# The first rows of the mixers' output product run under the long convolution, and product streams take in weights across their borders

## The reference, cut to what matters

```python
h = rms_norm_2(x, norm_g[l, 0])
q, k, v, g, lr, u_f, u_h, u_s = jnp.split(h @ w_in[l], split_at, axis=-1)
y_a = gla_mixer(q, k, v, g, lr, ...)                     # linear attention
y_b = rms_norm_2(fnet_mixer(u_f), grp_norm_g[l, 0])      # Fourier mixer
y_c = rms_norm_2(hyena_mixer(u_h, ...), grp_norm_g[l, 1])   # two long convolutions
y_d = rms_norm_2(shortconv_mixer(u_s, ...), grp_norm_g[l, 2])
mix = jnp.concatenate([y_a, y_b, y_c, y_d], axis=-1)     # 4 x 512 columns
x = x + mix @ w_out[l]
x = x + cross_attention(rms_norm_2(x, ...), rms_norm_2(mem, mem_norm_g), w_xq, w_xkv, w_xo)
x = x + swiglu(rms_norm_2(x, norm_g[l, 2]), w_gate_up, w_down)
```

## Time and profile before

| what | value |
|---|---|
| median of three runs | 4070.18 us (4068.68 to 4078.13) |
| profiled execution | 4056.73 us |
| its span | 4054.9 us |
| TensorE busy | 3645.2 us, 90% |
| VectorE busy | 1987.7 us, 49% |
| ScalarE busy | 1517.0 us, 37% |
| mean granted TensorE clock | 0.948 of full speed |
| read from memory | 523.28 MB, 131 GB/s over the span |

### The profile page before, as it was taken

How to read it: one execution, slowest core, us unless ns; L and a number is a source line. 1 busy time by engine, 2 the same in 40 slices (tenths; PEclk the granted TensorE clock), 3 DMA queues, 4 the chain that set the end, 5 groups by cost and what they waited for, 6 DMA issues and landing times. The chain is left out here.

```text
span 4054.9 us, 73903 instructions
## 1 busy us (share of the span) xinstructions
PE 3645.2 (90%) x32796; PEld 2991.7 (74%) x32796; DVE 1987.7 (49%) x3429; ACT 1517.0 (37%) x2562; POOL 271.3 (7%) x321
## 2 busy tenths in 40 slices
PE   7899999999999978969989787968999989999998
PEld 3576676776777756847778677826889889999887
DVE  1444454444544455374565446545544455555444
ACT  1333333333433332154444343324443344444343
POOL 0011110100101130021000000010000000000000
PEclk8899999999999989979999799979999999999999
DMA  9523323333232343223225343305554445555554
GB/s 326 179 60 103 99 80 112 103 99 117 83 112 78 103 142 109 70 96 104 94 91 184 108 154 115 104 21 172 169 189 146 156 148 186 183 183 185 187 187 156
DMA packets 343100, 536.18 MB, mean 132 GB/s; under 512 B 11484, under 2 KB 119676, under 8 KB 340604
## 3 DMA queue, kind: packets, MB, share of 16 engines
q1 hardware_dynamic: 340476, 527.25, 40.4%
q10 hardware_dynamic: 2304, 4.20, 0.3%
HBM read 523.28 MB, written 8.13 MB: 131 GB/s over the span
## 5 line engine op out<-in xcount | busy, mean ns | idle before, releaser
L300 PE MATMUL lane<-r,r 128*128 128x256 f32 (+1 forms) x8664 | 1554.9, 328 | 31.7 <-DVE r L258 16.8
L300 PEld LDWEIGHTS lane<-r,r 128*128 128x128 f32 x8664 | 1300.7, 190 | 215.4 <-issue 24.8
L300 PE MATMUL bank<-r,r 128*128 128x512 f32 (+2 forms) x6216 | 1363.6, 357 | 54.8 <-DVE r L258 44.3
L258 DVE TENSOR_TENSOR r<-ring,r 128x1024 fp32r<-128x1024 f32 x749 | 913.7, 1227 | 998.1 <-ACT r L297 997.1
L300 PEld LDWEIGHTS bank<-r,r 128*128 128x128 f32 x6216 | 1016.8, 195 | 259.0 <-issue 65.1
L297 ACT ACTIVATE r<-ring 128x1024 fp32r<-128x1024 f32 x749 | 785.8, 1056 | 1070.6 <-PE lane L300 683.5
L300 PE MATMUL lane<-arena 64*64 64x64 f32 (+5 forms) x13676 | 663.2, 250 | 90.4 <-DVE arena L258 33.5
L300 PEld LDWEIGHTS lane<-arena 64*64 64x64 f32 (+2 forms) x13676 | 502.8, 140 | 239.7 <-issue 124.0
L297 ACT ACTIVATE arena<-lane 128x256 f32<-128x256 f32 (+4 forms) x575 | 251.4, 456 | 582.9 <-PE lane L300 482.5
L269 DVE COPY arena<-lane 128x256 f32<-128x256 f32 (+2 forms) x365 | 131.5, 362 | 335.4 <-PE lane L300 332.3
L258 DVE TENSOR_TENSOR arena<-arena 128x256 f32<-128x256 f32 (+6 forms) x546 | 241.9, 475 | 33.6 <-ACT arena L297 13.7
(11 more groups left out here) (101 smaller groups left out, 1385.6 us busy)
## 6 DMA issues: line engine op xcount, KB each, us to landing
ring<-in_mod_w SPq DMA_DIRECT2D x96, 1024.0 KB, 5.3
ring<-in_w_gate_up SPq DMA_DIRECT2D x88, 1024.0 KB, 5.1
ring<-in_ev_w_in SPq DMA_DIRECT2D x44, 1024.0 KB, 8.6
ring<-in_w_down SPq DMA_DIRECT2D x44, 1024.0 KB, 5.1
ring<-in_od_w_in SPq DMA_DIRECT2D x40, 1024.0 KB, 5.1
ring<-in_w_in SPq DMA_DIRECT2D x40, 1024.0 KB, 5.2
ring<-in_w_xkv SPq DMA_DIRECT2D x32, 1024.0 KB, 5.2
ring<-in_ev_w_out SPq DMA_DIRECT2D x16, 1024.0 KB, 5.1
```

The costliest lines, as they stand in the source:

```text
L258: return Nothing() if self.e is None else self.e.tensor_tensor(o, a, b, op)
L300: return Nothing() if self.e is None else self.e.matmul(o, l, r, start=start, stop=stop)
```

## The change

- **Streams share one list of waiting units.** `stream` now only appends its units to `waiting`. Whoever runs a unit first prepares up to three waiting units, of whichever stream. The calls of `stream` stand earlier in the order, ahead of the drain of the stream before, at seven borders: before attention's input product, the linear attention's inputs, the inputs of short conv and Fourier mixer, the long convolution's inputs, the output product, the queries, and the feed-forward part. The stream of keys and values is created after the output product's units have all been placed.
- **The output product begins in the long convolution.** Its contraction now starts with mix tile 12 (`rot` 12: tiles 12 to 15, 0 to 7, then 8 to 11). Of column groups 0 and 1 the first twelve contraction tiles, 12 units in all, come first and are placed at the yields of the new generator `hyena()`. The tile splits of the mix that they need are placed there too.
- **Buffers and loads.** Instead of the fence "hyena" only a mark is set, on which SyncE's `hy_load` and ScalarE's mix splits wait. The high parts of the mix lie where the input rows were. The convolution takes its banks from four (4 to 7) and not eight. `load_ahead(6)` asks for three pieces of output weights ahead of `hy_load`. `load_mem` stands before the filters' transforms, goes to a place of its own (`M.memx`), and waits for no fence.

```diff
-    M.mF = Pair("mF", at(MF, 4096), at(GAP, 4096), KT, R)
+    M.mF = Pair("mF", at(MF, 4096), at(0, 4096), KT, R)
...
+    M.memx = at(4096, 4096).rearrange("p (t n) -> p t n", t=2)
...
-    def stream(groups, turn):
-        units = []
-        for g in groups:
+    waiting, ahead = [], [0]
+
+    def stream(groups, turn, first=(0, 0)):
+
+
+
+        stretches = [(g, k0, i >= first[0] or k0 >= first[1]) for i, g in enumerate(groups)
+                     for k0 in range(0, g.kt, 2 * min(g.kt, PIECE // 2 // g.n))]
+        count = 0
+        for g, k0, _ in sorted(stretches, key=lambda s: s[2]):
+            g.turn = turn
             hk = min(g.kt, PIECE // 2 // g.n)
-            for k0 in range(0, g.kt, 2 * hk):
-                m2 = min(2 * hk, g.kt - k0)
-                for h in range(0, m2, hk):
-                    units.append(Unit(g, k0 + h, min(hk, m2 - h), h, h + hk >= m2, numbers[0]))
-                    numbers[0] += 1
-                    units[-1].whole = (k0, m2)
-        at_hand = [None]
-
-        def prepare(u):
-            g = u.group
-            if u.half == 0:
...
-        for u in units[:2]:
-            prepare(u)
+            m2 = min(2 * hk, g.kt - k0)
+            for h in range(0, m2, hk):
+                u = Unit(g, k0 + h, min(hk, m2 - h), h, h + hk >= m2, numbers[0])
+                numbers[0] += 1
+                u.whole = (k0, m2)
+                waiting.append(u)
+                count += 1
 
         def run():
-            for i, u in enumerate(units):
-                if i + 2 < len(units):
-                    prepare(units[i + 2])
+            for _ in range(count):
+                while ahead[0] < min(3, len(waiting)):
+                    prepare(waiting[ahead[0]])
+                    ahead[0] += 1
+                u = waiting.pop(0)
+                ahead[0] -= 1
                 products(u)
                 for _ in range(CHORES[0] if len(u.group.tiles) == 4 and not u.group.feats else CHORES[1]):
                     if chores and next(chores[0], 0) == 0:
                         chores.pop(0)
                 yield 1
         return run()
+
+    at_hand = [None]
+
+    def load_ahead(n):
+
+        for u in waiting[:n]:
+            g = u.group
+            if u.half == 0 and u.piece is None:
+                u.piece = piece(g.w, None, (u.whole[0] + g.rot) % g.kt, u.whole[1], g.c0, g.n)
+
+    def prepare(u):
+        load_ahead(ahead[0] + 1)
+        if u.half == 0:
+            at_hand[0] = u.piece
+        u.piece = at_hand[0]
+        step("split_w", u)
+
+    def products(u):
+        g = u.group
+        if u.k == 0:
+            g.banks = [bank(g.turn) for _ in g.tiles]
+        step("times_w", u)
+        if u.k + u.m == g.kt:
+            for b, f in zip(g.banks, g.tiles):
+                step(g.kind, b, f, *g.args)
+            if g.done:
+                g.done()
...
-    drain(fill)
+    out_first = fill
...
                   + [rows("gF", KT, [0, 1], "od_w_out", n * 512, 512, "add_second", (n,),
                           (lambda: step("load_ln1")) if n == 0 else None) for n in range(4)], st_turn)
+    drain(out_first)
     step("rope_load")
     step("norm0", [2, 3])
     step("norm0", [0, 1])
...
     step("attended")
+    to_gla = stream([rows("hF0", KT, [0, 1], "w_in_2", W2_LR, 32, "lr_in", (), lambda: step("lr_turned", bank(aux))),
+                     feats("hF0", KT, "w_in_2", 0, "qk_in")]
+                    + [rows("hF0", KT, [0, 1], "w_in_2", W2_V + 512 * n, 512, "vg_in", (n,)) for n in range(2)], st_turn)
     drain(fill)
     step("norm1")
...
     drain(normed("hF0", "xk", 0, turn_all, ("norm1",)))
     step("load_mix")
-    drain(stream([rows("hF0", KT, [0, 1], "w_in_2", W2_LR, 32, "lr_in", (), lambda: step("lr_turned", bank(aux))),
-                  feats("hF0", KT, "w_in_2", 0, "qk_in")]
-                 + [rows("hF0", KT, [0, 1], "w_in_2", W2_V + 512 * n, 512, "vg_in", (n,)) for n in range(2)], st_turn))
+    fill = stream([feats("hF0", KT, "w_in_2", W2_S + 512 * n, "us_in", (n,)) for n in range(3)]
+                  + [feats("hF0", KT, "w_in_2", W2_F, "uf_in")], st_turn)
+    drain(to_gla)
     step("gla_ready")
...
-    fill = stream([feats("hF0", KT, "w_in_2", W2_S + 512 * n, "us_in", (n,)) for n in range(3)]
-                  + [feats("hF0", KT, "w_in_2", W2_F, "uf_in")], st_turn)
     weave(gla(), fill, 1.1)
+    to_hyena = stream([feats("hF0", KT, "w_in_2", W2_H + 512 * n, "uh_in", (n,)) for n in range(3)], st_turn)
     drain(fill)
     step("fence", "mixers")
...
-    fill = stream([feats("hF0", KT, "w_in_2", W2_H + 512 * n, "uh_in", (n,)) for n in range(3)], st_turn)
-    weave(local_mixers(), fill, 1.5)
-    drain(fill)
+    weave(local_mixers(), to_hyena, 1.5)
+    fill = stream([rows("mF", KT, [0, 1], "w_out_2", n * 512, 512, "add_x", ("x3", n, None),
+                        (lambda: step("x3_done")) if n == 3 else None, 12) for n in range(4)], Turn([0, 1, 2, 3]), (2, 12))
+    hy_turn = Turn([4, 5, 6, 7])
+    drain(to_hyena)
     step("local_done")
-    fill = stream([rows("mF", KT, [0, 1], "w_out_2", n * 512, 512, "add_x", ("x3", n, None),
-                        (lambda: step("x3_done")) if n == 3 else None) for n in range(4)], st_turn)
-    step("fence", "hyena")
+    step("mark", "hyena")
+    load_ahead(6)
     step("hy_load")
-    step("hy_one", bank(turn_all))
...
+    early = [12, 13, 14, 15, 0, 1, 2, 3, 4, 5, 6, 7]
+
+    def splits(n):
+        for _ in range(n):
+            step("split", "mF", early.pop(0))
+
+    def hyena():
+        splits(4)
+        yield 1
+        splits(2)
+        yield 1
+        step("hy_one", bank(hy_turn))
+        splits(2)
+        yield 1
+        step("hy_two", bank(hy_turn))
+        splits(2)
+        yield 1
+        splits(2)
         for tl in range(2):
-            step("hy_sides", o, tl)
-    for m, side_ in (("hc", 0), ("hb", 1), ("hd", 0)):
+            for n in range(4):
+                step("hy_taps", tl, n, bank(hy_turn))
         for o in range(2):
+            for tl in range(2):
+                step("hy_sides", o, tl)
+        yield 1
+        step("load_mem")
+        for m, side_ in (("hc", 0), ("hb", 1), ("hd", 0)):
+            for o in range(2):
+                for f in range(2):
+                    step("hy_filter", m, side_, o, f, bank(hy_turn))
+        step("fence", "conv")
+        for tl in range(2):
+            for n in range(3):
+                step("hy_rows", tl, n, bank(hy_turn))
+        step("load_skip")
+        for o in range(2):
+            yield 1
+            for m in ("hc", "zi"):
+                for f in range(2):
+                    step("hy_there", o, m, f, bank(hy_turn))
             for f in range(2):
-                step("hy_filter", m, side_, o, f, bank(turn_all))
-    step("fence", "conv")
-    for tl in range(2):
-        for n in range(3):
-            step("hy_rows", tl, n, bank(turn_all))
-    step("load_skip")
-    for o in range(2):
-        for m in ("hc", "zi"):
-            for f in range(2):
-                step("hy_there", o, m, f, bank(turn_all))
-        for f in range(2):
-            step("hy_times", o, f)
-        step("hy_back", o, [bank(turn_all), bank(turn_all)])
-    for tl in range(2):
-        step("hy_norm", tl)
-    for j in range(0, 4, 2):
-        step("to_mix", "hyena", 1, j, bank(turn_all))
+                step("hy_times", o, f)
+            yield 1
+            step("hy_back", o, [bank(hy_turn), bank(hy_turn)])
+        for tl in range(2):
+            step("hy_norm", tl)
+        yield 3
+        for j in range(0, 4, 2):
+            step("to_mix", "hyena", 1, j, bank(hy_turn))
+
+    weave(hyena(), fill)
     step("fence", "mixed")
-    for k in range(KT):
+    for k in range(8, 12):
         step("split", "mF", k)
-    step("load_mem")
-    next(fill)
     weave(normed("mT", "memr", "mem_g", aux, ("mem",)), fill, 2)
+    kv = stream([feats("mT", KT, "w_xkv_2", 512 * n, "kf_in", (n,)) for n in range(4)]
+                + [rows("mT", KT, [0, 1], "w_xkv_2", D + 512 * n, 512, "vr_in", (n,)) for n in range(4)], st_turn)
     drain(fill)
     step("mem_done")
 
 
-    fill = stream([feats("mT", KT, "w_xkv_2", 512 * n, "kf_in", (n,)) for n in range(4)]
-                  + [rows("mT", KT, [0, 1], "w_xkv_2", D + 512 * n, 512, "vr_in", (n,)) for n in range(4)], st_turn)
-    next(fill)
-    weave(normed("hF16", "xk", 16, aux, ("x3",)), fill, 1)
-    drain(fill)
-    step("kv_done")
+    next(kv)
+    weave(normed("hF16", "xk", 16, aux, ("x3",)), kv, 1)
 
...
     fill = stream([feats("hF16", KT, "w_xq_2", 512 * n, "xq_in", (n,), q_ready(n)) for n in range(4)]
                   + [rows("oF", KT, [0, 1], "w_xo_2", n * 512, 512, "add_x", ("x4", n, 0)) for n in range(4)], st_turn)
+    drain(kv)
+    step("kv_done")
...
-    drain(fill)
-    step("x4_done")
-
-
-    drain(normed("hF32", "xk", 32, turn_all, ("x4",), summed=True))
-    step("ff_go")
...
```

(12 more changed lines are left out.)

45 lines of the change are left out of this document (19 added, 26 removed).

## The result

The changed kernel took 4017.76 us (median of four runs, 4010.66 to 4024.18) beside 4069.43 us of the kernel before: a ratio of 0.9868, with a 95% interval of 0.9846 to 0.989. A second set of runs gave 4013.02 and 0.9874 (0.9857 to 0.989). Forecast were 4021 and a range of 4006 to 4050.

What follows compares the result with a forecast made beforehand. TensorE, busy 90% of the span, was taken as the bound, so gains lie where it idles or runs slow. Convolution and tail 36.3 plus borders 13.0 give 49.3 us off the 4070.18 median: 4021 us, range 4006 to 4050.

Steps and rivals of the forecast that it cites:

- The convolution's share: Long convolution and output product: tail 39.7 us shorter, less a start 3.4 late, gives 36.3 us gained.
- The lateness walk: Long convolution with 12 units in it: step-by-step delay against the old chain, ending with the tail 3.4 us late.
- the waits at the memory norm: Output product's tail: two norm steps ahead of the splits of units 14 and 16, waits 2.0 and 1.1 us.
- The 4.6 us stand: Output product's start: TensorE's wait for weights behind 2 MB of memory input, expected to go.
- The borders: Five stream borders: earlier first splits remove waits, 2.3 + 2.8 + 1.7 + 2.3 + 3.9 = 13.0 us, bounds 8 to 18.
- The moved parts that I cost at nothing: Mix's second place, earlier memory rows, pieces asked for before filter constants, skip row's load: no added time.
- The first rival: Long convolution: clock stays low between the groups, tail starts 28 us late, 4045 us; chance 0.24.
- The second rival: Long convolution: no unit fits the gaps, each added in full at the lower clock, 67.2 us, 4085; chance 0.05.
- Borders alone: Whole kernel: the convolution gives back what the tail gains, only borders count, 4057 us; chance 0.07.
- Better: Whole kernel: lateness nil and borders at 18 us, 4012 us or less; chance 0.04.
- The two rules weighed in the prediction: TensorE's throttled clock is the default and activity releases it; ScalarE's and VectorE's queues are strictly first-in first-out.
- about 54: Total gain in us if the chain could pass the guests' splits ahead of the second sine and first exponential.

Runs made afterwards that it cites:

- no_guests: first_early with no output-product unit and no mix tile split inside the long convolution; all 32 units and 16 splits follow it: 4037.2 us, 0.9928.
- after_again: The changed kernel, unedited, run again: 4013.02 us, 0.9874 of the kernel before.
- first_early: Changed kernel, plus the first stream (even block's output weights) preparing its first two units at creation, ahead of the pool loads: 4002.25 us, 0.9849.
- old_borders: first_early with lookahead cut at each stream's end, except into the output product, and first units prepared at the old places: 4031.3 us, 0.9914.
- all_front_none: first_early with keys' stream created earlier, guests moved into taps and spectral waits, none ahead of first filter matmul, three before last transposes: 3994.64 us, 0.9835.
- mid_taps: first_early with one output-product unit between the fourth and fifth of eight taps and none at the transposed rows: 4011.84 us, 0.9869.
- memory_late: first_early with the memory rows' load moved below the fence behind the long convolution: 4006.58 us, 0.9867.

## Why the prediction was right, and where it was not

- **The convolution's share, 36.3 forecast, 37.3 measured.** The lateness walk held at its steps: first filter matmul 4.4 (measured 4.5), first tap 8.3 (7.0), filters 5.3 (4.9), second inverse transform 0.3 (1.4), last transposes 4.3 (4.8), tail 3.4 (4.2). The tail was 62.0 for 64.0: of the waits at the memory norm, put at 2.0 and 1.1, 0.4 is left.
- **Two of its terms had wrong reasons, so part of the agreement at the steps is luck.** The walk was made from the chain of the kernel before and did not see that the moved `mark` lets that chain start 2.3 us sooner. Against no_guests the two units in front cost 7.0 and not 4.4. And the taps, put at a pace of 0.97 "with TensorE kept busy", ran mostly at the lower level (0.64 of the clock in their window). The start of the filters came out right for another reason. TensorE's own first tap was only 4.3 us late (22.6 behind the last input product for 18.3), while VectorE's was 7.0: TensorE filled four banks ahead of it. The first eight tap matmuls then took 0.8 less (6.21 for 7.01), a bank was waited for 1.2, and the last eight took 0.2 more: 4.9.
- **The 4.6 us stand.** It was put down to weights behind the memory input, and in the trace of before that was so (6.48 of ScalarE's wait). no_guests has a stand of nearly the same length with every load at hand, which the change's own order makes: tile splits and norm pass ahead of the weight split. The walk priced the norm steps, at 2.0 and 1.1, but not tile splits in front of them; in after 0.4 is left, with twelve of the sixteen splits moved away.
- **The borders, 13.0 forecast, about 20 measured** by the stages of before and after (1.8 + 10.0 + 2.2 + 5.9; 21.1 with after_again), 18.4 between first_early and old_borders. It is also above the stated upper bound of 18. Mis-sized are the terms of the linear-attention inputs (2.8, measured 6.4 to 7.8) and of the feed-forward (3.9, measured 6.6 to 7.3); the clock was left out of both, although the upper bound named it for the first. The border that was to stay stayed: 2.01 both times.
- **The step that failed by omission:** "The moved parts that I cost at nothing" lists no first stream. That `stream` no longer prepares at its call was read as a gain at five borders, and not followed to the one call where the first unit is taken much later: 11.2 us lost.
- **The total** came out 3 us from the median since the border's surplus (+7) and the first stream (-11) nearly cancel. The right total is in part luck; the 36 of the convolution is borne out by no_guests.
- **The first rival**, a clock that stays low among the guests, is out: 0.88 in the convolution for 0.75, and 1.00 in the filters, though not the "above 0.9" that was to show it. Its kernel of truth is the taps. The second rival needed 4.4 us of lateness a unit; the measured is 8.6 for twelve (125.0 against 116.4), 0.7 each. Borders alone is out by no_guests. Better (4012 or less) had the borders right, at 18 and more, but not its nil lateness.
- **The two rules weighed in the prediction.** That activity releases the lower level agrees where units stand among the transforms. It does not agree for two other operations: the tap matmuls ran 14.02 us without a gap at 0.50, and the 32-column product fell to 0.50 with TensorE busy throughout. There the measurement decides. The strict order of the queues agrees: taking the guests' splits out of the sine steps brought the first tap 4.7 us forward. The sum "about 54" of that paragraph takes 2.2 us off ahead of the second sine where the walk has 1.3 (4.4 to 5.7); it would be about 53.

## What to carry to other kernels

Work put into the gaps of a serial chain is cheap in the middle, where the bounding engine waits for others, and dear at its head, where all of the chain waits behind it: two units there cost 7 us, and twelve placed elsewhere cost none in all_front_none. When a helper that prepares at its call becomes lazy, look at every call for what stands between the call and its first use; one such place ate a fifth of the gain. And a wait at the same place and of nearly the same length in two kernels need not be the same wait: look at what released it in each.

## What the runs showed of the hardware

Two groups of matmuls ran without a gap and stayed at the lower level to their end: sixteen tap matmuls with 64 rows of weights (14.02 us at a granted clock of 0.50) and 96 matmuls of 32 columns (busy 20.63 of 20.63 us at 0.50). A unit of 128-row, 512-column matmuls between the taps (4.09 us in mid_taps) was followed by a second half of 3.70 us instead of 7.19.

Being entered at the upper level was not always enough to keep it. The taps kept it in all_front_none (3.70 us for eight, clock 1.00, behind 0.99 us of idle and with a unit between the halves). In after, behind 1.82 us of idle, they began at it and fell to the lower one 1.0 us later; behind 2.94 they were at the lower one from the start (7.01 us for eight). The 32-column product of after began at it and fell 4.8 us later, though TensorE had not idled since the transposes. Windows of after's taps:

```profile
2657.41:2658.40 0.99, 0.99 (x3) 0.51 (x4) 0.00 (x0) 0.99 (x1) 0.00 (x0) 1.00 0.03 8
2659.00:2671.97 12.97, 11.80 (x15) 3.89 (x13) 7.68 (x12) 9.67 (x15) 0.00 (x0) 0.50 0.00 0
```

Stages of unchanged code wander by a few us between executions: gate and up took 513.5 to 518.3 us in kernels that do not differ there, cross-attention's output 109.2 to 109.4, or 112.3 in two runs. In gate and up the groups follow each other at 46.14 us; in memory_late (513.5) three of them came after 44.76, in first_early (518.3) none, which is 4.1 of the 4.8 between them.
